# A hybrid attention trunk on one core: TensorE transposes probabilities before the value products of the same step

## What is computed

```python
hn = rms_norm(h, norm_mix_pre[i])
if i % 2 == 0:   # even layer: 8 heads of latent attention, 8 heads of forgetting attention
    mix = even_mixer(hn, ...)
else:            # odd layer: dilated windows (3 groups x 4 heads), native sparse attention (4 heads)
    mix = odd_mixer(hn, ...)
h = h + rms_norm(mix, norm_mix_post[i])
m = jnp.square(jax.nn.relu(rms_norm(h, ...) @ w_mlp_up[i])) @ w_mlp_down[i]
h = h + rms_norm(m, norm_mlp_post[i])
h = h + sigmoid(rms_norm(h, ple_norm[i]) @ w_ple_gate[i]) * (p[i] @ w_ple_proj[i])
```

## Time and profile before

| | |
|---|---|
| median of 3 runs | 3223.07 us (3221.32 to 3223.57) |
| span of the profiled execution, first to last instruction | 3221.5 us |
| instructions | 37112 |
| mean granted TensorE clock, share of full speed | 0.958 |

### The profile page before, as it was taken

The page is one execution under the profiler, slowest core; times in us unless marked ns, Lnnn a source line. Parts: engine busy times, 40 slices in busy tenths (PEclk is TensorE's granted clock), DMA queues, the critical chain, the costliest instruction groups (busy, mean ns, idle before and its releaser), DMA issues.

```text
span 3221.5 us, 37112 instructions
## 1 busy us (share of the span) xinstructions
PE 2919.4 (91%) x13684; PEld 2385.4 (74%) x13684; DVE 1331.0 (41%) x1905; ACT 860.2 (27%) x1581; POOL 952.7 (30%) x622
## 2 busy tenths in 40 slices
PE   8896888889999999999999976867889999999999
PEld 5785777767888888876788865757658888888867
DVE  4625777325222222227433147787272222222264
ACT  3204766322110000024200035756331000011141
POOL 2320144342332332252232202131423223323342
PEclk9998999999999999999999986879989999999999
DMA  4236432211111111111235264544201111111112
GB/s 154 109 126 178 124 80 66 79 40 33 46 52 46 46 47 51 46 53 53 79 124 218 79 162 102 120 103 120 79 33 46 52 46 46 48 50 46 59 35 77
DMA packets 73791, 253.66 MB, mean 79 GB/s; under 512 B 9699, under 2 KB 13283, under 8 KB 73367
## 3 DMA queue, kind: packets, MB, share of 16 engines
q1 hardware_dynamic: 58728, 196.35, 20.5%
q10 hardware_dynamic: 14944, 55.74, 4.5%
HBM read 203.99 MB, written 52.78 MB: 80 GB/s over the span
## 4 chain that ended last, share of the span: by engine, by line
PE 75%; DVE 15%; issue 4%; ACT 3%; DMA 2%; POOL 1%; SPq 0%; DVEq 0%; ACTq 0%; POOLq 0%
PE ACC L1035 62%; PE OP L1197 3%; PE ACC L1167 3%; PE TR L1181 3%; DVE R L1634 2%; DVE T L1657 1%; DVE H L1660 1%; DVE PT L1783 1%; PE OP L1091 1%; DVE XL L1640 1%; ACT PT L1431 1%; PE TR L1210 1%; DVE T L1682 1%; DVE PB L1772 1%; DVE HL L1685 1%
## 5 line engine op out<-in xcount | busy, mean ns | idle before, releaser
L873 POOL CAST WH<-RAW 128x1024 fp32r<-128x1024 f32 x203 | 215.9, 1064 | 1575.5 <-PE ACC L1035 1554.6
L1035 PE MATMUL ACC<-XH,WH 128*128 128x512 f32 x1792 | 575.0, 402 | 72.3 <-DVE XL L1640 38.5
L1035 PE MATMUL ACC<-XL,WH 128*128 128x512 f32 x1792 | 556.4, 392 | 0.0
L1035 PE MATMUL ACC<-XH,WL 128*128 128x512 f32 x1792 | 555.4, 391 | 0.0
L875 POOL TENSOR_TENSOR WL<-RAW,WH 128x1024 fp32r<-128x1024 f32 x203 | 495.2, 2439 | 24.8 <-POOL WH L873 1.5
L1035 PEld LDWEIGHTS ACC<-XH,WH 128*128 128x128 f32 x1792 | 337.3, 189 | 172.8 <-issue 89.6
L1035 PEld LDWEIGHTS ACC<-XL,WH 128*128 128x128 f32 x1792 | 339.2, 189 | 71.8
L1035 PEld LDWEIGHTS ACC<-XH,WL 128*128 128x128 f32 x1792 | 338.8, 189 | 71.7
L1393 ACT ACTIVATE HH<-T 128x1024 fp32r<-128x1024 f32 x64 | 67.9, 1061 | 1168.6 <-DVE T L1682 1168.6
L1689 DVE TENSOR_TENSOR M<-M,ACC 128x1024 f32<-128x1024 f32 x128 | 156.3, 1221 | 496.1 <-PE ACC L1035 496.1
L1035 PE MATMUL ACC<-HH,WH 128*128 128x512 f32 x1024 | 316.8, 391 | 17.0 <-DVE HL L1685 17.0
(11 more groups left out here) (192 smaller groups left out, 3466.8 us busy)
## 6 DMA issues: line engine op xcount, KB each, us to landing
RAW<-in_w SPq DMA_DIRECT2D x203, 512.0 KB, 3.4
QK<-y_odds SPq DMA_DIRECT2D x128, 256.0 KB, 5.2
y_odds<-HALVES ACTq DMA_DIRECT2D x16, 1024.0 KB, 5.2
QK<-y_foxs SPq DMA_DIRECT2D x48, 256.0 KB, 5.4
y_foxs<-HALVES ACTq DMA_DIRECT2D x8, 1024.0 KB, 5.2
y_kv<-Q ACTq DMA_DIRECT2D x8, 512.0 KB, 2.6
BIAS<-y_f SPq DMA_DIRECT2D x8, 512.0 KB, 7.7
H<-in_xT ACTq DMA_DIRECT2D x8, 512.0 KB, 7.3
```

Source lines behind the costliest of these rows:

```text
L873: nc.gpsimd.tensor_copy(WH[:, slot], RAW[:, slot]).then_inc(s_whi, 1)
L1035: mm = nc.tensor.matmul(acc[:, h * HALF:(h + 1) * HALF], w(k), x[:, k, h * HALF:(h + 1) * HALF], start=first and k == k0 and w is ws and x ...
```

## The change

Inside each attention step TensorE issues the transposes of task s - 2 ahead of the value products, where it issued them behind. Nothing is added or removed, and the lists of the other engines and every semaphore count stay as they are.

```diff
--- before.py
+++ after.py
@@ -1216,10 +1216,10 @@
                         turn_v(st.start)
                     if st.logits:
                         logits(st.logits)
+                    if st.turn:
+                        turn(st.turn)
                     if st.values:
                         values(st.values)
-                    if st.turn:
-                        turn(st.turn)
                     if st.norm:
                         turn_spread(st.norm)
                 pe.wait_ge(s_ttr, ph.end.tasks)
```

## The result

The changed kernel takes 3311.16 us (median of 4 runs, 3308.26 to 3316.37). The kernel before, run beside it, takes 3223.32 (4 runs, 3221.32 to 3228.41). The ratio is **1.0274** (95% interval 1.0260 to 1.0288): 88 us slower. The forecast was 3238, 15 us slower, with a range up to 3252. The direction was right. The size was not, and none of the three rivals reaches it. The profiled execution took 3316.37 us, 5 us above that median, so sums over its trace are a little large against the 88 us.

What follows compares the result with a forecast made beforehand. Bound taken: TensorE, 91% busy, with VectorE setting the pace through two transpose banks in part of each attention head. Large jobs 14 us plus small jobs 1 made 15, on 3223 giving 3238 us; range 3222 to 3252.

Steps and rivals of the forecast that it cites:

- What bounds the stages: Order matters only in the attention stages; VectorE sets the pace from the transposes of task 4 to those of task 7.
- x8 at i = 0: Large jobs, scores(0) step: eight value products move behind task 6's transposes, into TensorE's 0.88 us wait before task 7; cost 0.
- x16 at i = 4: Large jobs, scores(4) step: sixteen value products behind task 2's transposes; bank free, blocks 1.9 us earlier but scores(5) unchanged; 0.
- x12 at i = 2: Large jobs, scores(2) step: twelve value products wait behind task 0's transpose for a bank; `fox` 0.8 us late, only head e = 1.
- x4 at i = 6: Large jobs, scores(6) step: four value products delay scores(7) by 0.5 us; covered in `fox`, costs 0.5 per `mla` head.
- the upper bound: 0.5 us for the four products in `fox`, `sel` and `win` too, 0.83 per small half: 28 us, or 3251.
- Small jobs: Twelve halves with spread sums, each between -0.35 and +0.83 us, taken as 0.1; `cmp` 0; in all 1 us.
- Job by job: Large jobs get longer: `fox` and `sel` 0.8 us each, `mla` 1.7, `win` 1.2; 14.0 us over all.
- Rival 1: ScalarE's copies of task 6's blocks start sooner, each of twelve large jobs gains 0.9 us: 3212; chance 0.09.
- Rival 2: No change: TensorE's waits only change places because VectorE bounds each whole job: 3223; chance 0.17.
- Rival 3: More idle time brings a stretch at the lower clock into each of twelve large jobs: 34 us, or 3257; chance 0.09.

Runs made afterwards that it cites:

- x8 alone: Changed order only in the large jobs' step with scores(0), two PT buffers, against the kernel before: 3266.34 us, ratio 1.0147.
- three buffers: A third buffer for the turned probabilities PT added to the changed order, against the kernel before: 3236.76 us, ratio 1.0042.
- x16 moved: Changed order only in the large jobs' step with scores(4), two PT buffers, against the kernel before: 3221.56 us, ratio 0.9995.

## Why the prediction was right or wrong

- **What bounds the stages.** Right: only the attention stages changed, and VectorE does set the pace behind scores(0): x8 alone delays the copy by 1.28 us in a head and costs as much in ten of the twelve heads e = 1.
- **x8 at i = 0, "I take 0".** This is the step that failed, with 41.4 of the 88 us. Its reasoning on TensorE (the bank sets the start, x8 moves into the 0.88 us wait) is right, and with three buffers x8 measured 3221.60, 3 below before. What it lacks is the question who waits for x8. The forecast priced TensorE's waits for a bank, and never asked about `s_pv`, which x8 raises and on which ScalarE's copy in this very step waits. In place of the 0, the runs show that copy 1.27 us late behind x8, 50.6 us of its waits in 24 heads, and nothing left of the 41.4 once the third buffer takes the wait away.
- **x16 at i = 4, 0.** The size is right (-2.5 us), but the reason given is half wrong. With two buffers ScalarE does not get these blocks 1.9 us earlier; it starts on them when it did before, since it waits for x16 either way. With three it starts 1.76 us earlier.
- **x12 at i = 2, in all 10.0.** Measured 12.7. The bank wait that was forecast as 0.8 is there with 0.66, with two buffers and with three, and it makes the cost: 11.6 us lie in the heads e = 1, as forecast, and 10.8 stay there with three buffers. The copy waits for x12 in the heads e = 0 too, where it starts hardly later and costs hardly anything.
- **x4 at i = 6, in `mla` only, 4.0.** Measured 13.3, beyond the upper bound as well: that let x4 cost 0.5 in each of the other eight jobs, 8.0 in all, although it counted `mla` twice a job, once for each head. Here too the copy (of task 4) waits for x4, a delay that was priced only for the scores behind x4. With three buffers 4.1 is left, 3.5 of it in `mla`: without the buffer wait this term was right.
- **Small jobs, 1.** Measured 15.4, beyond the bound of +10. Here too the copies wait on the products, 53.1 us in 44 places in the trace of that run, which no row of the kernel before shows. In the trace of the changed order with three buffers their stretch is only 2.3 us longer than before, against 17.2 in that of this run, so most of the 15.4 is the buffer's. (The old order with three buffers has the same 2.3.)
- **Job by job.** Without the buffer wait the forecast holds: with three buffers the `fox` job shown is 0.5 longer (0.8 forecast) and the `mla` job 1.5 (1.7 forecast), and the whole is 12 us longer (15 forecast). That the whole comes so close is in part luck: its terms for x12 and x4 are there with 14.9 us in the large jobs, and other stretches of these jobs, which the forecast left alone, are 7 us shorter. With the buffer wait the `fox` job is 5.3 and the `mla` job 8.6 longer.
- **Rival 1, copies start sooner.** It has the right place, ScalarE's copy of task 6, and the wrong sign: VectorE gets that copy 1.27 later. **Rival 2** falls. **Rival 3, the clock,** is true as a follower. The granted clock is 0.943 against 0.958, and TensorE is busy 46.9 us longer for the same instructions. With three buffers the clock is 0.958 again, so the clock did not fall by the order itself but with the buffer wait. How the 88 us divide into wait and clock stays open. The 46.9 us are an estimate of the most that it can be, since part of them may stand beside other waits.
- **The range.** Its upper end came from the bounds of costs that the forecast knew. A wait that had never been seen waiting had no row, and so no bound.

## What to carry to other kernels

When instructions move back in an engine's order, list first every semaphore that they raise and who waits on it, not only what they and their new neighbours wait for. A double buffer is such a semaphore: its release is invisible in a profile as long as it comes early, and it becomes the bound when the consumer is put behind the producer of the next filling. Before such a change is judged, give the buffer one more slot. Here that turned +88 us into +12 and cost the old order nothing, which told the cause in two runs.

A new releaser in the list of waits is not a cost by itself. Sum the waits of the instruction over all its releasers, or ask whether it starts later: with x16 moved the copy had 38.0 us of waits of a new kind and 172.1 in all, where it had 172.0.

## What the runs showed of the hardware that was not expected

The clock fell in a job in which TensorE never stood idle for more than 1.6 us at a time: at the place shown above it waited 1.56 us and then 1.54, and x12 ran at half the clock (2.60 us against 1.35). Before, waits of 1.08 and 1.54 stood at the same place and the clock stayed full, so the idle time at this place alone hardly tells the two apart. In the changed kernel x8, a few us earlier, already ran at a granted clock of 0.51 (510.90 to 512.84). What brought the clock down there was not tested. The third `fox` job had waits of 1.00 and 1.22 and stayed at full clock in a stretch of 25 us around them:

```profile
390.00:415.00 25.00, 19.06 (x137) 16.72 (x135) 18.62 (x43) 16.82 (x39) 2.51 (x3) 1.00 0.37 87
```
